# A two-layer decoder trunk on one core: squares of the new x in PSUM, one slab fetched ahead, and a bias copy cut in eight and moved

## The chip, the cores and the metric

The kernel runs on one core of a Trainium2 chip. The metric is the time of the program on the device in microseconds (us), smaller is better. The kernel before ran three times; its median is 1198.24 us.

## What is computed

Two decoder layers on 512 tokens of width 1024, in float32. Layer 0 mixes tokens with an indexer's sparse attention, layer 1 with a sliding window of 128 keys and sinks. Each is followed by a SwiGLU feed-forward part of width 2816, and the whole ends in a norm. One table of relative-position biases serves both mixers.

```python
def rms_norm(x, g):
    xf = x.astype(jnp.float32)
    y = xf * lax.rsqrt(jnp.mean(xf * xf, axis=-1, keepdims=True) + EPS)
    return (y * g.astype(jnp.float32)).astype(x.dtype)
...
    for layer in range(DEPTH):
        h = rms_norm(x, attn_norm[layer])
        if layer % N_MIXERS == 0:
            x = x + dsa_mixer(h, a_w_in[j], a_latent_norm[j], a_w_uv[j], a_w_out[j], rel_bias)
        else:
            x = x + swa_mixer(h, b_w_in[j], b_b_in[j], b_sinks[j], b_w_out[j], b_b_out[j], rel_bias)
        h = rms_norm(x, ffn_norm[layer])
        x = x + swiglu(h, ffn_w_gate_up[layer], ffn_w_down[layer])
    return rms_norm(x, final_norm)
```

## The kernel before

**Layout.** x is held transposed in SBUF, as 8 tiles of 128 features by 512 tokens, m = 0 to 7. Each float32 product is made of three TensorE products of 128x128 by 128x512: hi times hi, lo times hi and hi times lo (`mm3`, L570 to L572), where hi is the value rounded to fp32r and lo the rest.

**Slabs.** Weights come in 100 slabs, numbered in the order of use, into the two slots of `raw` (slot n % 2). SyncE (SP) issues each as two DMAs (`slab`, L308 and L309). Before it does, it waits on `lo_done` until the slab two before has been split. ScalarE (ACT) makes `w_hi` of a slab (`split_half`, L1043) once it has landed and the `w_hi` slot is free, GpSimd (POOL) makes `w_lo` (L461), and TensorE (PE) then has two output tiles of it (`unit_done`). A slab of the down products gives half a tile. Names: `S_F0` = 15 and `S_F1` = 62 are the first slabs of the gate and up products, `S_BK` = 53 holds layer two's keys and values, `S_BQ` = 54 to 57 its queries, `S_BO` = 58 to 61 its output projection. All of these DMAs go through SP's one queue, in the order in which SP issues them.

**Seams.** Between two parts of a layer the new x is made tile by tile. For each m VectorE (DVE) adds PE's result to x (L1605 and L1617 for the two output projections, L1654 for the down products), ACT makes `xs_hi` = x times gain (L1058) and the square of x (L1064, into `sq_mem` in SBUF), and DVE makes `xs_lo` (L1400) and adds the square to `ss` (L1409). PE starts the next part with `first_tiles`, which takes `xs_lo` m by m, and then `norm_sum` (L618) sums `ss` over the partitions. In the first norm, on the input, the squares go to PSUM instead (L1104, L1447). ACT, DVE and POOL run each program strictly in order. In the seam after the down products of layer 0, ACT splits slab 54 (`S_BQ`) before it makes `xs_hi` of m = 7. SP waits until PE has ended all down products (`unit_done`, `U_BK`) before it issues `sink` (L408), because `sink` lies where `act_hi` lay, and slab 54 is issued after that.

**The bias in DRAM.** `bias_row` holds one row of 1024 values per head. Skewed copies of it, DRAM to DRAM, make `bias_toep`, 128 rows of 512 values for each of the 16 heads. For layer 0 SP issues four copies of 4 heads (L381), between slabs. For layer 1, whose rows have 256 values, it issues one copy of all 16 heads (L402), between the last slab of layer 0's output projection and `S_F0`. Layer 1's attention reads from it two heads at a time into `b_toep` (`pair_in`, L421): DVE's `b_lowest` (L1740) takes `b_toep` and PE's logits, ACT takes the exponents. The attention runs over k = 0 to 7, two heads each. PE does, in this order, `b_logits(k)` (L579), the transposes of k - 2 (`b_turn`, L914 and L917), and in halves the query product of k + 2 (`b_project`). `b_logits(k)` waits until `b_lowest(k - 1)` has emptied its PSUM banks.

```python
            sp.wait_ge(neg_done, 4 * H)
            skew_b = bass.AP(tensor=bias_row.tensor, offset=ROW_A + P - 1, ap=[[GLEN, H], [-1, P], [1, 2 * P]])
            sp.dma_start(bias_toep[:, :, 0:2 * P], skew_b).then_inc(toep_out, 16)
            feed_forward(0, S_F0, S_D0)
...
            sp.wait_ge(toep_out, 32)
            pair_in(0)
```

Of the kernel before, what the change touches and what calls it, by code (L numbers as in the profile page):

```python
# [7 lines left out]
F32 = mybir.dt.float32  # L8
F32R = mybir.dt.float32r
ALU = mybir.AluOpType  # L10
ACT = mybir.ActivationFunctionType

P = 128
D = 1024
T = 512
DM = D // P
NB = T // P
FF = 2816
FT = FF // P
H = 16  # L20
R = 128
DH = 64
# [16 lines left out]
ROW_A, ROW_B = 640, 384  # L39
GLEN = ROW_A + ROW_B  # L40
# [4 lines left out]
U_A1, U_A2, U_AO, U_F0, U_D0 = 0, 6, 22, 30, 74  # L45
U_BK, U_BQ, U_BO, U_F1, U_D1, U_END = 90, 92, 100, 108, 152, 168
SLOT = 2048
KD = FT // 2
CUT_WIDE, CUT_DOWN = (1024, 2048), (768, KD * P)

# [13 lines left out]
    return value  # L64

SQ_BANK = (4, 5, 7)
B_OUT_BANK = (4, 1, 2, 3, 0, 1, 2, 3)

def is_down(n):
# [19 lines left out]
def trunk(nc, x_in, rel_bias, par_in, a_w_in, a_w_uv, a_w_out, b_w_in, b_sinks, b_w_out,  # L89
          w_gate_up, w_down, consts, bias_row, bias_toep, out):  # L90
    ctx = ExitStack()
    with ctx:
        def sb(name, shape, dt=F32, where=ctx):
            return where.enter_context(nc.sbuf_tensor(name, shape, dt))

        def sem(name):
            return ctx.enter_context(nc.semaphore(name))
# [25 lines left out]
        ss = sb("ss", [P, T])  # L123
# [87 lines left out]
        fm = ExitStack()  # L211
        act_hi = sb("act_hi", [P, FT, T], F32R, fm)
        act_lo = sb("act_lo", [P, FT, T], F32R, fm)
        gate = sb("gate", [P, T], F32, fm)
        up = sb("up", [P, T], F32, fm)
        glu = sb("glu", [P, 2, T], F32, fm)
# [11 lines left out]
        GAIN = [G_ATTN[0], G_FFN[0], G_ATTN[1], G_FFN[1]]  # L228

        raw_full = [sem("raw_full0"), sem("raw_full1")]  # L230
        hi_done, lo_done = sem("hi_done"), sem("lo_done")
        unit_done = sem("unit_done")
        id_in, tab_in, small_in, sink_in = sem("id_in"), sem("tab_in"), sem("small_in"), sem("sink_in")
# [53 lines left out]

        def pieces(buf, n):

            if S_BQ <= n < S_BO:  # L290
                if buf is raw:
                    v = buf[:, n % 2, :].rearrange("p (k a j c) -> p a k j c", k=DM, a=2, j=2)
                else:
                    v = buf[:, n % 2, :].rearrange("p (k j a c) -> p a k j c", k=DM, a=2, j=2)
                return [v[:, a, :, :, :] for a in range(2)]
            cut = CUT_DOWN if is_down(n) else CUT_WIDE
            return [buf[:, n % 2, 0:cut[0]], buf[:, n % 2, cut[0]:cut[1]]]
# [4 lines left out]
        def _(sp):  # L302
            def slab(n, it, src):

                for dst, s in src(n % 2):
                    if n >= 2:

                        sp.wait_ge(lo_done, 2 * (n - 1) + 4 * it)  # L308
                    sp.dma_start(dst, s).then_inc(raw_full[n % 2], 16)  # L309
# [28 lines left out]
            def feed_forward(layer, s_gu, s_d):  # L338

                w = w_gate_up[layer]  # L340
                with sp.Fori(0, FT // 2) as i:
                    for v in range(2):
                        slab(s_gu + v, i, two_halves(w, (2 * i + v) * P, (2 * i + v) * P + FF))
                with sp.Fori(0, DM) as m:
                    for c in range(2):
                        slab(s_d + c, m, down(w_down[layer], c, m))

# [48 lines left out]
                toep_in(h)  # L396
            for n in range(S_AO + 2, S_F0):
                slab(n, 0, wide(a_w_out[0], (n - S_AO) * 256))

            sp.wait_ge(neg_done, 4 * H)  # L400
            skew_b = bass.AP(tensor=bias_row.tensor, offset=ROW_A + P - 1, ap=[[GLEN, H], [-1, P], [1, 2 * P]])
            sp.dma_start(bias_toep[:, :, 0:2 * P], skew_b).then_inc(toep_out, 16)  # L402
            feed_forward(0, S_F0, S_D0)

            slab(S_BK, 0, wide(b_w_in[0], H * DH))

            sp.wait_ge(unit_done, U_BK)
            sp.dma_start(sink[:, :], b_sinks[0:1, :].broadcast_to([P, H])).then_inc(sink_in, 16)  # L408
# [1 line left out]
            for n in range(S_BQ, S_BO):  # L410
                c0 = (n - S_BQ) * 2 * DH
                slab(n, 0, two_halves(b_w_in[0], c0, c0 + H // 2 * DH))

            def pair_in(j):

# [16 lines left out]
                                 b_w_out[0, a * 512:(a + 1) * 512, c0:c0 + 256]  # L432
                                 .rearrange("(k p) n -> p k n", p=DH)).then_inc(raw_full[n % 2], 16)

            sp.wait_ge(toep_out, 32)
            pair_in(0)
            pair_in(1)
            bo_slab(S_BO)
# [588 lines left out]
        def _(act):  # L1027
# [5 lines left out]
            def split_half(n, half, it=0, after=0):  # L1033
                if half == 0 and n == 0:

                    act.wait_ge(raw_fore, 32)
                elif half == 0 or n == 0:

                    act.wait_ge(raw_full[n % 2], 32 * (n // 2 + 1) + 32 * it)
                    if n >= 2:  # L1040

                        act.wait_ge(unit_done, after)
                nc.scalar.copy(pieces(w_hi, n)[half], pieces(raw, n)[half]).then_inc(hi_done, 1)  # L1043
# [5 lines left out]
            def new_x(e, m, par, gain=None):  # L1049

                c = DM * e + m
                n0 = held(act, c + 1)
                n1 = held(act, c - 1)
                act.wait_ge(tab_in, TAB)

                act.wait_ge(x_new, n0)
                if gain is not None:
                    nc.scalar.activation(xs_hi_m(m), x[:, m, :], ACT.Copy,  # L1058
                                         scale=params[:, bass.ds(gain + m, 1)]).then_inc(xhi_done, 1)
                if e > 0 or m >= 2:  # L1060

                    act.wait_ge(tab_in, TAB)
                    act.wait_ge(ss_done, n1)
                nc.scalar.activation(sq[:, par, :], x[:, m, :], ACT.Square).then_inc(sq_done, 1)  # L1064

            def xs_hi_m(m):
                return xs_hi[:, bass.ds(m * T, T)]
# [322 lines left out]
        def _(dve):  # L1390
# [3 lines left out]
            def new_x(e, m, par, gain=None):  # L1394
# [11 lines left out]
                if not (isinstance(c, int) and c == 0):  # L1406

                    dve.wait_ge(ss_done, c)
                nc.vector.tensor_tensor(ss[:, :], ss[:, :], sq[:, par, :], ALU.add).then_inc(ss_done, 1)  # L1409

            def norm(e):

# [399 lines left out]
```

## Time and profile before

| | before |
|---|---|
| runs | 1200.09, 1198.24, 1195.34 us; median 1198.24 |
| the profiled execution: its own time | 1199.46 us |
| its span, first to last instruction | 1197.7 us |
| PE busy | 1164.0 us (97%) |
| DVE busy | 563.3 us (47%) |
| ACT busy | 457.8 us (38%) |
| POOL busy | 613.7 us (51%) |
| mean granted TensorE clock | 0.994 |

The span is the time between the first and the last instruction. The device time is 1.8 us longer. Busy times are sums over the whole span. The PE figure counts modelled ends of pipelined matmuls. A matmul is shown with a duration of about 390 ns, while one starts about every 0.23 us.

### The profile page before, as it was taken

What the parts mean: (1) busy time and instruction counts of PE and PEld (TensorE: products, weight loads), DVE (VectorE), ACT (ScalarE), POOL (GpSimd) and SP (SyncE); (2) the same over time, 40 slices, a digit from 0 to 9 for tenths busy, and PEclk for the clock granted to TensorE, in tenths of its full rate; (3) what the DMA queues carried; (4) which work ended last, traced back from release to release, by engine and by line L of the source; (5) the groups of instructions that cost most, each with busy time, mean ns of one, the idle gap of its engine ahead of it and who ended that gap; (6) DMA issues with size and microseconds to landing.
All of it is one profiled execution on the core that took longest, in us unless ns stands there. A gap on an engine that the chain in (4) does not pass through costs nothing.

```text
span 1197.7 us, 16046 instructions
## 1 busy us (share of the span) xinstructions
PE 1164.0 (97%) x5600; PEld 963.0 (80%) x5600; DVE 563.3 (47%) x927; ACT 457.8 (38%) x849; POOL 613.7 (51%) x359
## 2 busy tenths in 40 slices
PE   7999999999999999999999999999999999999996
PEld 5767889987788888888888778887888888888885
DVE  5379867745644434442222476647444444421111
ACT  5343257752422332223222376634323322332232
POOL 4435757864444544444444487834445444534441
PEclk9999999999999999999999999999999999999998
DMA  7531401118333233322332442313332333233221
GB/s 209 173 134 53 141 27 48 51 55 157 106 105 97 79 104 105 97 71 82 96 96 83 119 102 58 76 36 106 106 103 76 101 105 103 65 92 97 86 83 71
DMA packets 181283, 112.46 MB, mean 94 GB/s; under 512 B 7308, under 2 KB 175559, under 8 KB 181240
## 3 DMA queue, kind: packets, MB, share of 16 engines
q1 hardware_dynamic: 180512, 110.68, 33.2%
q10 hardware_dynamic: 728, 1.22, 0.3%
q8 instruction: 25, 0.41, 0.1%
q14 instruction: 18, 0.15, 0.0%
HBM read 109.72 MB, written 8.45 MB: 99 GB/s over the span
## 4 chain that ended last, share of the span: by engine, by line
PE 81%; DVE 5%; issue 4%; ACT 3%; DMA 2%; POOL 1%; ACTq 0%; SPq 0%; DVEq 0%
PE ps L570 26%; PE ps L572 25%; PE ps L571 25%; DVE ss L1409 2%; DMA raw<-in_ffn_w_gate_up 2%; PE ps L579 2%; PE ps L785 1%; ACT w_hi L1043 1%; DVE work L1505 1%; PE ps L914 1%; PE ps L764 1%; POOL w_lo L461 1%; DVE work L1489 1%; ACT xs_hi L1058 1%; DMA raw<-in_b_w_in 1%
## 5 line engine op out<-in xcount | busy, mean ns | idle before, releaser
L461 POOL TENSOR_TENSOR w_lo<-raw,w_hi 128x1024 fp32r<-128x1024 f32 (+1 forms) x200 | 462.7, 2335 | 497.5 <-ACT w_hi L1043 488.9
L570 PE MATMUL ps<-xs_hi,w_hi 128*128 128x512 f32 (+3 forms) x1024 | 399.3, 390 | 7.8 <-DVE xs_lo L1400 2.5
L572 PE MATMUL ps<-xs_hi,w_lo 128*128 128x512 f32 (+3 forms) x1024 | 394.8, 386 | 0.0
L571 PE MATMUL ps<-xs_lo,w_hi 128*128 128x512 f32 (+3 forms) x1024 | 394.6, 385 | 0.0
L1043 ACT CAST w_hi<-raw 128x1024 fp32r<-128x1024 f32 (+1 forms) x196 | 178.9, 962 | 433.8 <-PE ps L572 414.1
L570 PEld LDWEIGHTS ps<-xs_hi,w_hi 128*128 128x128 f32 x1024 | 192.5, 188 | 53.4 <-DVE xs_lo L1400 3.8
L571 PEld LDWEIGHTS ps<-xs_lo,w_hi 128*128 128x128 f32 x1024 | 192.6, 188 | 38.8 <-issue 1.1
L572 PEld LDWEIGHTS ps<-xs_hi,w_lo 128*128 128x128 f32 x1024 | 192.4, 188 | 38.8
L570 PE MATMUL ps<-act_hi,w_hi 128*128 128x512 f32 x352 | 139.2, 396 | 0.0
L572 PE MATMUL ps<-act_hi,w_lo 128*128 128x512 f32 x352 | 138.0, 392 | 0.0
L571 PE MATMUL ps<-act_lo,w_hi 128*128 128x512 f32 x352 | 136.6, 388 | 0.0
L1637 DVE TENSOR_TENSOR glu<-std,up 128x512 f32<-128x512 f32 x44 | 67.7, 1540 | 77.0 <-ACT std L1232 76.8
L1640 DVE TENSOR_TENSOR act_lo<-glu,act_hi 128x512 f32 (+1 forms) x44 | 76.2, 1731 | 41.5 <-ACT act_hi L1237 41.5
L1633 DVE TENSOR_TENSOR up<-ps,rstd 128x512 f32<-128x512 f32 x44 | 30.4, 692 | 138.7 <-PE ps L572 138.7
L1654 DVE TENSOR_TENSOR x<-ps,x 128x512 f32 x16 | 11.1, 692 | 175.0 <-PE ps L572 175.0
L572 PEld LDWEIGHTS ps<-act_hi,w_lo 128*128 128x128 f32 x352 | 66.1, 188 | 15.5
L571 PEld LDWEIGHTS ps<-act_lo,w_hi 128*128 128x128 f32 x352 | 66.1, 188 | 14.5
L570 PEld LDWEIGHTS ps<-act_hi,w_hi 128*128 128x128 f32 x352 | 66.2, 188 | 13.0
L553 POOL TENSOR_SCALAR b_prob<-b_prob,b_rinv 128x128 f32<-128x128 f32 (+1 forms) x64 | 54.1, 870 | 11.2 <-DVE b_rinv L1718 11.1
L1409 DVE TENSOR_TENSOR ss<-ss,sq_mem 128x512 f32<-128x512 f32 x32 | 55.2, 1725 | 9.8 <-ACT sq_mem L1064 9.8
L1237 ACT CAST act_hi<-glu 128x512 f32 (+1 forms) x44 | 27.4, 622 | 76.9 <-DVE glu L1637 76.9
L1400 DVE SCALAR_TENSOR_TENSOR xs_lo<-x,params,xs_hi (+1 forms) x24 | 25.4, 1060 | 49.0 <-ACT xs_hi L1058 49.0
(182 smaller groups left out, 1361.0 us busy)
## 6 DMA issues: line engine op xcount, KB each, us to landing
raw<-in_ffn_w_gate_up SPq DMA_DIRECT2D x88, 512.0 KB, 4.9
raw<-in_ffn_w_down SPq DMA_DIRECT2D x32, 384.0 KB, 3.6
raw<-in_a_w_in SPq DMA_DIRECT2D x20, 512.0 KB, 4.9
raw<-in_ffn_w_down SPq DMA_DIRECT2D x32, 320.0 KB, 4.0
raw<-in_b_w_in SPq DMA_DIRECT2D x10, 512.0 KB, 5.1
bias_toep<-bias_row SPq DMA_DIRECT2D x4, 1024.0 KB
toep<-bias_toep SPq DMA_DIRECT2D x16, 256.0 KB, 2.6
raw<-in_a_w_out SPq DMA_DIRECT2D x8, 512.0 KB, 4.3
```

The lines of the kernel that those rows point to most:

```text
L461: nc.gpsimd.tensor_tensor(pieces(w_lo, n)[half], pieces(raw, n)[half], pieces(w_hi, n)[half].bitcast(F32), ALU.subtract)\
L553: nc.gpsimd.tensor_scalar(at, at, b_rinv[:, k % 2, a, i:i + 1], None, ALU.mult)\
L570: nc.tensor.matmul(dst, wh, xh, start=start, stop=False, **kw)
L571: nc.tensor.matmul(dst, wh, xl, start=False, stop=False, **kw)
L572: return nc.tensor.matmul(dst, wl, xh, start=False, stop=stop, **kw)
L1043: nc.scalar.copy(pieces(w_hi, n)[half], pieces(raw, n)[half]).then_inc(hi_done, 1)
L1237: nc.scalar.copy(act_hi[:, j + 2 * it, :], glu[:, j % 2, :]).then_inc(ah_done, 1)
L1400: nc.vector.scalar_tensor_tensor(xs_lo[:, bass.ds(m * T, T)], x[:, m, :], params[:, bass.ds(gain + m, 1)], xs_hi[:, bass.ds(m * T, T)].bit ...
L1409: nc.vector.tensor_tensor(ss[:, :], ss[:, :], sq[:, par, :], ALU.add).then_inc(ss_done, 1)
L1633: nc.vector.tensor_tensor(up[:, :], ps[:, b + 1, :], rstd[:, :], ALU.mult).then_inc(up_done, 1)
L1637: nc.vector.tensor_tensor(glu[:, v, :], silu[:, :], up[:, :], ALU.mult).then_inc(glu_done, 1)
L1640: nc.vector.tensor_tensor(act_lo[:, v + 2 * it, :], glu[:, v, :], act_hi[:, v + 2 * it, :].bitcast(F32), ALU.subtract)\
```

## The change

Three things, at the places where one part of a layer follows another.

- The squares of the new x go to two banks of PSUM (`NORM_SQ`, a pair for each of the four norms) instead of `sq_mem`, and DVE adds them to `ss` from there.
- Slab 53 (`S_BK`) is fetched into a buffer of its own, `raw_next`, which lies where the feed-forward part's `gate`, `up` and `glu` lay. It is issued after the down slabs of the first three m, and slab 55 then waits for slab 51 instead of slab 53.
- The copy of `bias_row` for layer 1 leaves its place ahead of `S_F0`. It is cut into eight copies of two heads, two behind each of the slabs 54 to 57. SP waits for all eight before `pair_in(0)`.

```diff
--- before.py
+++ after.py
@@ -45,6 +45,7 @@
 U_A1, U_A2, U_AO, U_F0, U_D0 = 0, 6, 22, 30, 74
 U_BK, U_BQ, U_BO, U_F1, U_D1, U_END = 90, 92, 100, 108, 152, 168
 SLOT = 2048
+AHEAD = 3
 KD = FT // 2
 CUT_WIDE, CUT_DOWN = (1024, 2048), (768, KD * P)
 
@@ -64,6 +65,7 @@
     return value
 
 SQ_BANK = (4, 5, 7)
+NORM_SQ = {1: (4, 5), 2: (2, 3), 3: (5, 7), 4: (2, 3)}
 B_OUT_BANK = (4, 1, 2, 3, 0, 1, 2, 3)
 
 def is_down(n):
@@ -211,6 +213,9 @@
         fm = ExitStack()
         act_hi = sb("act_hi", [P, FT, T], F32R, fm)
         act_lo = sb("act_lo", [P, FT, T], F32R, fm)
+        next_m = ExitStack()
+        raw_next = sb("raw_next", [P, SLOT], F32, next_m)
+        next_m.close()
         gate = sb("gate", [P, T], F32, fm)
         up = sb("up", [P, T], F32, fm)
         glu = sb("glu", [P, 2, T], F32, fm)
@@ -228,6 +233,7 @@
         GAIN = [G_ATTN[0], G_FFN[0], G_ATTN[1], G_FFN[1]]
 
         raw_full = [sem("raw_full0"), sem("raw_full1")]
+        raw_ahead = sem("raw_ahead")
         hi_done, lo_done = sem("hi_done"), sem("lo_done")
         unit_done = sem("unit_done")
         id_in, tab_in, small_in, sink_in = sem("id_in"), sem("tab_in"), sem("small_in"), sem("sink_in")
@@ -287,6 +293,8 @@
 
         def pieces(buf, n):
 
+            if buf is raw and n == S_BK:
+                return [raw_next[:, 0:CUT_WIDE[0]], raw_next[:, CUT_WIDE[0]:CUT_WIDE[1]]]
             if S_BQ <= n < S_BO:
                 if buf is raw:
                     v = buf[:, n % 2, :].rearrange("p (k a j c) -> p a k j c", k=DM, a=2, j=2)
@@ -303,7 +311,10 @@
             def slab(n, it, src):
 
                 for dst, s in src(n % 2):
-                    if n >= 2:
+                    if n == S_BK + 2:
+
+                        sp.wait_ge(lo_done, 2 * (S_BK - 1))
+                    elif n >= 2:
 
                         sp.wait_ge(lo_done, 2 * (n - 1) + 4 * it)
                     sp.dma_start(dst, s).then_inc(raw_full[n % 2], 16)
@@ -341,7 +352,18 @@
                 with sp.Fori(0, FT // 2) as i:
                     for v in range(2):
                         slab(s_gu + v, i, two_halves(w, (2 * i + v) * P, (2 * i + v) * P + FF))
-                with sp.Fori(0, DM) as m:
+                for m in range(AHEAD):
+                    for c in range(2):
+                        slab(s_d + c, m, down(w_down[layer], c, m))
+                if layer == 0:
+                    v = raw_next[:, :].rearrange("p (k n) -> p k n", k=DM)
+                    g = b_w_in[0].rearrange("(k p) n -> p k n", p=P)
+
+                    sp.wait_ge(al_done, FT)
+                    for i in range(2):
+                        sp.dma_start(v[:, 4 * i:4 * i + 4, :], g[:, 4 * i:4 * i + 4, H * DH:H * DH + 256])\
+                            .then_inc(raw_ahead, 16)
+                with sp.Fori(AHEAD, DM) as m:
                     for c in range(2):
                         slab(s_d + c, m, down(w_down[layer], c, m))
 
@@ -396,13 +418,7 @@
                 toep_in(h)
             for n in range(S_AO + 2, S_F0):
                 slab(n, 0, wide(a_w_out[0], (n - S_AO) * 256))
-
-            sp.wait_ge(neg_done, 4 * H)
-            skew_b = bass.AP(tensor=bias_row.tensor, offset=ROW_A + P - 1, ap=[[GLEN, H], [-1, P], [1, 2 * P]])
-            sp.dma_start(bias_toep[:, :, 0:2 * P], skew_b).then_inc(toep_out, 16)
             feed_forward(0, S_F0, S_D0)
-
-            slab(S_BK, 0, wide(b_w_in[0], H * DH))
 
             sp.wait_ge(unit_done, U_BK)
             sp.dma_start(sink[:, :], b_sinks[0:1, :].broadcast_to([P, H])).then_inc(sink_in, 16)
@@ -410,6 +426,13 @@
             for n in range(S_BQ, S_BO):
                 c0 = (n - S_BQ) * 2 * DH
                 slab(n, 0, two_halves(b_w_in[0], c0, c0 + H // 2 * DH))
+                if n == S_BQ:
+
+                    sp.wait_ge(neg_done, 4 * H)
+                for h in (2 * (n - S_BQ), 2 * (n - S_BQ) + H // 2):
+                    skew_b = bass.AP(tensor=bias_row.tensor, offset=h * GLEN + ROW_A + P - 1,
+                                     ap=[[GLEN, 2], [-1, P], [1, 2 * P]])
+                    sp.dma_start(bias_toep[h:h + 2, :, 0:2 * P], skew_b).then_inc(toep_out, 16)
 
             def pair_in(j):
 
@@ -432,7 +455,7 @@
                                  b_w_out[0, a * 512:(a + 1) * 512, c0:c0 + 256]
                                  .rearrange("(k p) n -> p k n", p=DH)).then_inc(raw_full[n % 2], 16)
 
-            sp.wait_ge(toep_out, 32)
+            sp.wait_ge(toep_out, 64 + 8 * 16)
             pair_in(0)
             pair_in(1)
             bo_slab(S_BO)
@@ -1036,7 +1059,10 @@
                     act.wait_ge(raw_fore, 32)
                 elif half == 0 or n == 0:
 
-                    act.wait_ge(raw_full[n % 2], 32 * (n // 2 + 1) + 32 * it)
+                    if n == S_BK:
+                        act.wait_ge(raw_ahead, 32)
+                    else:
+                        act.wait_ge(raw_full[n % 2], 32 * (n // 2 + 1 - (n > S_BK and n % 2)) + 32 * it)
                     if n >= 2:
 
                         act.wait_ge(unit_done, after)
@@ -1061,7 +1087,7 @@
 
                     act.wait_ge(tab_in, TAB)
                     act.wait_ge(ss_done, n1)
-                nc.scalar.activation(sq[:, par, :], x[:, m, :], ACT.Square).then_inc(sq_done, 1)
+                nc.scalar.activation(ps[:, NORM_SQ[e][par], :], x[:, m, :], ACT.Square).then_inc(sq_done, 1)
 
             def xs_hi_m(m):
                 return xs_hi[:, bass.ds(m * T, T)]
@@ -1406,7 +1432,7 @@
                 if not (isinstance(c, int) and c == 0):
 
                     dve.wait_ge(ss_done, c)
-                nc.vector.tensor_tensor(ss[:, :], ss[:, :], sq[:, par, :], ALU.add).then_inc(ss_done, 1)
+                nc.vector.tensor_tensor(ss[:, :], ss[:, :], ps[:, NORM_SQ[e][par], :], ALU.add).then_inc(ss_done, 1)
 
             def norm(e):
 
```

On SP, ahead of the gate and up slabs of layer 0, the order before is this (`L402` is the copy of 16 heads, its rows times values stand behind the names):

```order
L389 DMA toep<-bias_toep 128x512 x14
L309 DMA raw<-in_a_w_out 128x4x256 x4
L402 DMA bias_toep<-bias_row 2048x1x256
L341 UNCONDITIONAL_BRANCH
L341 ISA
L309 ISA
L309 DMA raw<-in_ffn_w_gate_up 128x8x128
```

In the changed kernel the same place reads:

```order
L411 DMA toep<-bias_toep 128x512 x14
L320 DMA raw<-in_a_w_out 128x4x256 x4
L352 UNCONDITIONAL_BRANCH
L352 ISA
L320 ISA
L320 DMA raw<-in_ffn_w_gate_up 128x8x128
```

The copy is gone from between the two kinds of slabs. The second place is SP after the down products of layer 0, before:

```order
L309 DMA raw<-in_b_w_in 128x4x256 x2
L408 DMA sink<-in_b_sinks 128x16
L309 DMA raw<-in_b_w_in 128x8x128 x8
L421 DMA b_toep<-bias_toep 128x256 x4
L431 DMA raw<-in_b_w_out 64x8x256 x2
```

and in the changed kernel:

```order
L424 DMA sink<-in_b_sinks 128x16
L320 DMA raw<-in_b_w_in 128x8x128 x2
L435 DMA bias_toep<-bias_row 256x1x256 x2
L320 DMA raw<-in_b_w_in 128x8x128 x2
L435 DMA bias_toep<-bias_row 256x1x256 x2
L320 DMA raw<-in_b_w_in 128x8x128 x2
L435 DMA bias_toep<-bias_row 256x1x256 x2
L320 DMA raw<-in_b_w_in 128x8x128 x2
L435 DMA bias_toep<-bias_row 256x1x256 x2
```

Slab 53 has moved up into the down products. Slab 54 still stands behind `sink`, and each query slab is now followed by two copies. `pair_in` follows behind the last of them.

## Rows read from the trace of the kernel before

**Rows 1.** The page, busy time and instructions of each engine.
```profile
PE 1164.0 (97%) x5600; PEld 963.0 (80%) x5600; DVE 563.3 (47%) x927; ACT 457.8 (38%) x849; POOL 613.7 (51%) x359
```
**Rows 2.** Waits of PE over the span: us in total, times, longest.
```profile
PE ps L570 <- DVE xs_lo L1400: 2.5, 2, 1.5
PE ps L570 <- DVE x L1605: 1.8, 1, 1.8
PE ps L618 <- DVE ss L1409: 1.1, 1, 1.1
```
**Rows 3.** Chain of waits, 255 to 320 us: start, us, what.
```profile
273.68 18.74 DMA raw<-in_ffn_w_gate_up
```
**Rows 4.** Timeline, SP, ACT and PE, first seam: start, us, instruction, idle before.
```profile
267.34 0.60 SPq L402 DMA_DIRECT2D bias_toep<-bias_row  x1
...
292.52 2.00 ACT L1043 CAST w_hi<-raw 128x1024 fp32r<-128x1024 f32 x2 [7.12 <-DMA raw<-in_ffn_w_gate_up]
...
300.06 0.51 PE L570 MATMUL ps<-xs_hi,w_hi 128*128 128x512 f32 x1 [1.75 <-DVE x L1605]
...
310.91 0.50 PE L570 MATMUL ps<-xs_hi,w_hi 128*128 128x512 f32 x1 [1.03 <-DVE xs_lo L1400]
```
**Rows 5.** Instructions on the tile ss: duration ns min/median/max, first and last start.
```profile
L1409 DVE TENSOR_TENSOR ss<-ss,sq_mem x32: 683/1676/2890, 269.4 to 1186.5; 128x512 f32<-128x512 f32 x32
L1447 DVE TENSOR_TENSOR ss<-ss,ps x8: 687/687/690, 24.9 to 30.4; 128x512 f32<-128x512 f32 x8
```
**Rows 6.** Timeline, SP and ACT, seam after the down products.
```profile
655.36 2.00 ACT L1043 CAST w_hi<-raw 128x1024 fp32r<-128x1024 f32 x2 [4.95 <-PE ps L572]
...
663.23 23.58 SPq L309 DMA_DIRECT2D raw<-in_b_w_in  x8
...
669.73 2.00 ACT L1043 CAST w_hi<-raw 128x1024 fp32r<-128x1024 f32 x2 [12.37 <-DMA raw<-in_b_w_in]
...
679.91 1.98 ACT L1043 CAST w_hi<-raw 128x1024 fp32r<-128x1024 f32 x2
...
688.75 1.99 ACT L1043 CAST w_hi<-raw 128x1024 fp32r<-128x1024 f32 x2 [0.85 <-PE ps L572]
```
**Rows 7.** The page, DMA issues of the copies: count, KB each.
```profile
bias_toep<-bias_row SPq DMA_DIRECT2D x4, 1024.0 KB
...
bias_toep<-bias_row SPq DMA_DIRECT2D x1, 2048.0 KB
```
**Rows 8.** Timeline, SP, first and last of the four copies of 4 heads.
```profile
28.38 0.80 SPq L381 DMA_DIRECT2D bias_toep<-bias_row  x1
...
63.25 2.37 SPq L381 DMA_DIRECT2D bias_toep<-bias_row  x1
```
**Rows 9.** Windows with these copies; the last columns are granted clock, DMA share, GB/s.
```profile
42.00:52.00 10.00, 9.29 (x40) 6.79 (x40) 4.41 (x8) 4.05 (x6) 4.76 (x2) 1.00 0.27 101
...
69.00:80.00 11.00, 11.00 (x57) 7.05 (x58) 6.63 (x8) 6.75 (x12) 5.21 (x3) 1.00 0.26 101
...
81.00:82.00 1.00, 1.00 (x8) 0.59 (x8) 1.00 (x1) 0.24 (x1) 0.69 (x1) 1.00 0.67 130
```
**Rows 10.** Windows with the copy of 16 heads, and with slabs 54 and 55.
```profile
272.00:287.00 15.00, 15.00 (x67) 12.29 (x67) 9.50 (x11) 5.63 (x8) 5.23 (x2) 1.00 1.03 129
...
664.00:672.00 8.00, 8.00 (x37) 6.57 (x36) 0.00 (x0) 2.27 (x3) 1.14 (x1) 1.00 1.02 254
```
**Rows 11.** Timeline, SP, DVE and PE, start of layer 1's attention.
```profile
686.85 2.72 SPq L421 DMA_DIRECT2D b_toep<-bias_toep  x4
...
693.42 0.34 DVE L1740 CUSTOM_DVE_ANT_0 b_prob<-ps,b_toep,nsink 128x128 f32<-128x128 f32 x1
...
697.47 0.33 PE L579 MATMUL ps<-bk_hi,bq_hi 64*128 64x128 f32 x2
```
**Rows 12.** Landing time of the DMAs of L421, all 16.
```profile
DMA to landing us min/median/max: 1.9/2.4/6.1
```
**Rows 13.** A window behind two gaps of PE (1.1 and 1.9 us).
```profile
764.00:768.00 4.00, 3.33 (x10) 2.67 (x10) 2.85 (x9) 1.98 (x9) 4.00 (x6) 0.58 0.97 194
```

## The prediction

> **What bounds the kernel now.** I began with the busy times: PE is busy 97% of the span [rows 1], so a stage gets faster only where PE's gaps get shorter, and any new gap of PE is added to the time in full. Then I read who makes PE wait [rows 2]. The places that this change touches cost 1.75 and 1.03 us in the seam before layer 0's feed-forward part [rows 4] and 1.1 us at `norm_sum` in the seam after the down products (third row of [rows 2]). That is all the change can win, 3.9 us. The chain of waits names the cause of the first seam: the first gate and up slab took 18.74 us from issue to landing [rows 3], because the bias copy of 16 heads was issued just ahead of it [rows 4]. ACT stood still 7.12 us for that slab, and the `xs_hi` behind it came late. Last I read the DMA shares, for what the copies do to the queue [rows 7 to 10].
>
> **Part 1, squares in PSUM.** Adding a square from `sq_mem` took 0.68 to 2.89 us on DVE, and 0.69 us in all 8 cases where the square was in PSUM [rows 5]. The slow ones lie beside POOL's subtractions. I take 0.69 for all 32. It saves DVE time in every seam, but PE feels it in one place alone, the 1.1 us at `norm_sum`. I count that at nothing, for a reason given in part 3: what comes after it waits for a DMA that starts at a fixed point before it. ACT's write to PSUM changes place only, and I count it at nothing; four banks that PE does not use at that time hold the squares.
>
> **Part 2, slab 53 ahead.** ACT's split of slab 53 did not wait for a DMA but for PE to free the `w_hi` slot (the cast at 655.36, [rows 6]). So the earlier fetch has nothing to shorten. The wait of this seam is ACT's 12.37 us for slab 54 (the cast at 669.73, [rows 6]), which is issued at 663.23 because SP waits for the end of the down products first. The order of SP in the changed kernel still has slab 54 behind `sink`, so this wait stays, and with it `xs_hi` of m = 7, which stands behind the split. I count the part at nothing. Its cover is ample: slab 53's two DMAs go in among the down slabs.
>
> **Part 3a, the copy leaves the first seam.** With nothing ahead of it the first gate and up slab lands long before ACT could take it, since PE frees the `w_hi` slot only about 5.5 us before the cast at 292.52. ACT then has `xs_hi` of m = 4 some 5 us earlier, and DVE is no longer late with x of m = 5. At the end of the seam `xs_lo` of m = 7 is needed after 42 products of the seven earlier m. PE starts one per 0.224 us (67 in 15.00 us [rows 10]), so 9.4 us after it starts at about 298, and it is ready about 7 us after that start. Both gaps go: **2.8 us won**. Nothing is late next there.
>
> **Part 3b, eight copies of two heads between the query slabs.** This is the term that decides.
>
> How many DMA engines does one copy use? A copy of 4 heads ran at a DMA share of 0.27 [rows 9], which is 4 of 16 engines. The copy of 16 heads ran at 1.03 [rows 10], all of them. One engine per head: a copy of 2 heads should use 2.
>
> Are they always the same ones? The four copies of 4 heads were issued from 28.38 to 63.25 [rows 8]. Each moved 1 MB [rows 7] at 101 GB/s [rows 9], so took 10.4 us. Had the last copy had engines of its own, it would have been over by about 63.3 + 4 + 10.4 = 78 us, and it would have added its share to that of the third. But the share stayed at 0.26 and never 0.5 in 69 to 80 us, and the stream ended in the window of 81 to 82 [rows 9]. Four copies in a row (42 us) and the parts of three slabs between them (3 us each) starting at 28.9 end at 80 us. So the copies take turns on the same engines, and a slab's part on those engines waits behind them.
>
> What does a copy of 2 heads take? An engine has 128 rows of 1 KB. A 2 KB row took 10.4 us / 128 = 81 ns. Slabs 54 and 55, in 512 byte rows, had 256 rows per engine in some 7.1 us [rows 10], 28 ns each. Between the two on a straight line 1 KB takes 46 ns, and a copy **5.8 us**. The lower bound is half of the 10.4 us, 5.2; the upper one the full 10.4, if the cost is per row. Further off lies the copy of 16 heads: 2.1 MB at 129 GB/s [rows 10] is 16.3 us for 128 rows of 1 KB on each engine. I take 5.8 because two engines are nearer to four than to sixteen, and four showed no crowding.
>
> The Trainium skill (DMA: Bandwidth & Descriptors, Specifications) says that an engine moves about 27 GiB/s and that transfers of 512 B or more run at line rate. By that a copy would take an estimated 4.5 us and the sum below would be 10 us less; the 16.3 us of the 16 heads speak against using it as it stands.
>
> The two engines then work without a break from 664.9, some 1.7 us after slab 54's issue [rows 6]: four slabs of 3.6 us (two in 7.1 us, as above) and eight copies of 5.8 us, 60.8 us, until 725.7. With 1.2 us for the last landing and its semaphore, SP passes its wait at 726.9. Two DMAs of `pair_in(0)` take 0.7 us to issue (a quarter of 2.72 each [rows 11]) and 2.4 us to land [rows 12]: `b_lowest(0)` starts at 730.0 instead of 693.4 [rows 11]. PE's `b_logits(1)` needs all but the last 0.8 us of its 3.1 us, so starts at 732.3 instead of 697.5 [rows 11]: **34.9 us lost** (34.8 and a little for the semaphore). All on the path: behind `b_logits(1)` PE has nothing else it may do, and PE was busy before.
>
> Other waits in that stretch are hidden by this one. Slab 55 lands at about 684.5 on the two engines (664.9 + 3.6 + 11.6 + 3.6 = 683.7) where ACT wanted it at 679.9, and slab 56 at about 700 where ACT wanted it at 688.75 [rows 6]. ACT has `kv`, the queries and the exponents queued behind these splits, PE the first logits, POOL its splits. All are done by 730. That is also why the 1.1 us of part 1 wins nothing: the queue of the two engines starts at the end of the down products, ahead of `norm_sum`.
>
> **Part 4, the clock.** Behind gaps of 1.1 and 1.9 us the granted clock was 0.58 in the next 4 us [rows 13], near the lower level of 1.2 GHz, which costs 1.7 us of work at full rate. A gap of some 30 us will do this at least once: **1.7 us lost**.
>
> **Sum.** Own time of the profiled execution 1199.5 - 2.8 + 34.9 + 1.7 = 1233.3. That execution lies 1.2 us above the median of the runs, so the forecast is **1232 us**. With copies of 5.2 us it is 1227, with copies of 10.4 us 1269. The parts of slabs and the moment of the start may be off by 4 us below that.
>
> **Rivals.**
>
> *All sixteen engines serve each copy (not slower).* A DMA of 2 heads might be cut finer than by heads. Then a pair of copies, 0.5 MB at 129 GB/s, takes 4.1 us. Slab 57 cannot be issued before 685.8, when slab 55 is split; the queue then ends slab 57 at 691.6 and its copies at 695.7, and `b_lowest(0)` starts at 700.0, 6.6 us late. PE had 1.8 us to spare, so loses 4.8: 1199.5 - 2.8 + 4.8 - 1.2 = 1200. It decides if the share in the copies is above 0.5. Against it is the 0.27 of four heads.
>
> *The copies run at the pace of slabs on all engines.* A pair takes 2 us. The last still stands behind slab 57, so `b_lowest(0)` starts at about 697, and PE loses 1.7: 1197. This is the best case; it shows that even then the change wins about 1 us, since the last pair is issued where `pair_in(0)` was before [rows 11]. Against it is that no copy from DRAM to DRAM went above 129 GB/s.
>
> *Copies as slow as the 16 heads.* 8 x 16.3 us instead of 46.4 adds 84 us: 1316. The same 1 KB rows speak for it, that only two engines work speaks against.
>
> *The change does not do what it says.* For slab 53 this is my forecast, in part 2. Were I wrong, and slab 54 came earlier, 1.5 us of PE's wait for `xs_lo` would go (part of the first row of [rows 2]), but it would not be seen behind the wait for the copies.
>
> One page speaks to the first two rivals, apart from the rows. The Trainium skill (DMA: Bandwidth & Descriptors, Why a DMA increments its semaphore by 16 and not by 1) says that a DMA gets the largest number of engines up to 16 that divides the slowest dimension of both its sides, and the lowest-numbered ones. That makes 4 for 4 heads, which the share of 0.27 agrees with, and it would make 2 for 2 heads, which no run yet shows.
>
> **How the numbers follow.** The forecast's case (two fixed engines, copies of 5.2 to 10.4 us) has 0.84, the slow copies 0.03, all engines 0.07, the pace of slabs 0.06. The range is that of the first case, 1223 to 1269, and holds 0.82. A measurement of this kernel can tell about 0.5%, 6 us, from no change. Slower by more than that: 0.84 + 0.03 = 0.87. Within it: 0.11 of the two middle rivals. Faster by over 0.5%: 0.02, since even the best case wins 1 us.
>
> **What would show it.** In the changed profile: adding the squares takes 0.69 us throughout; ACT's wait of 7.12 us and PE's gaps of 1.75 and 1.03 us are gone; PE reaches layer 0's last down product about 2.8 us earlier. Then, from about 670 to 723 us, the DMA share is near 0.13 with short peaks for slabs, SP waits for `toep_out` into the 720s, and PE has one gap of about 30 us ahead of `b_logits(1)`, with a clock near half behind it. It is wrong if the share in the copies is above 0.2, or if the queue is empty at 700 us.

## The result, and the profile after

The changed kernel takes 1223.74 us (median of 4 runs, 1222.44 to 1225.37), the kernel before 1197.28 in the same comparison. The ratio is 1.0219, with a 95% interval of 1.0198 to 1.0240: slower by about 26 us. The forecast was 1232, with a range of 1223 to 1269 us: the measured time lies in it, 0.7 us above its lower end.

| | before | after |
|---|---|---|
| the profiled execution: its own time | 1199.46 | 1225.04 |
| its span | 1197.7 | 1223.2 |
| PE busy | 1164.0 | 1164.0 |
| DVE busy | 563.3 | 529.9 |
| mean granted TensorE clock | 0.994 | 0.984 |

The page of the changed kernel, busy time of each engine, answers to [rows 1]:

```profile
PE 1164.0 (95%) x5600; PEld 964.2 (79%) x5600; DVE 529.9 (43%) x927; ACT 457.1 (37%) x849; POOL 610.5 (50%) x359
```

PE does the same work in the same busy time, so the 25.5 us of span are gaps, nearly all of them in one place. Who makes PE wait, in us in total, times and longest, answers to [rows 2]:

```profile
PE ps L602 <- DVE b_low L1766: 27.2, 2, 26.2
...
PE ps L602 <- DVE bq_lo L1715: 4.2, 1, 4.2
```

The three waits of [rows 2] that the change could reach are gone, but for 1.67 us at `xs_lo` in the seam after the down products (1.46 before). One gap of 26.2 us has come, ahead of `b_logits(1)`, and 4.2 us ahead of `b_logits(0)` where there were 1.1. In sum: 26.2 + 3.1 + 0.2 more, 1.75 + 1.03 + 1.1 less, which is 25.6 us. The chain of waits through it (start, us, what):

```profile
685.64 8.36 DMA raw<-in_b_w_in
694.02 1.06 ACT w_hi L1069
...
704.91 13.78 DMA bias_toep<-bias_row
718.70 0.34 SPq L444
719.08 2.30 DMA b_toep<-bias_toep
...
723.94 2.93 PE ps L602 x24
```

Read it backwards: PE's logits wait for DVE, DVE for `b_toep`, SP's issue of that for the last bias copy, which took 13.78 us from issue to landing. Windows in which the copies alone moved data, but for the last rows of slab 54 in the first (granted clock, DMA share, GB/s last), beside [rows 9, 10]:

```profile
666.00:672.00 6.00, 4.33 (x19) 3.27 (x19) 1.85 (x2) 3.10 (x4) 4.15 (x2) 1.00 0.14 50
...
706.00:718.00 12.00, 0.00 (x0) 0.00 (x0) 0.00 (x0) 0.00 (x0) 0.00 (x0) 0.50 0.14 48
```

A share of 0.14 is 2.2 of 16 engines, and 256 KB at 48 GB/s take 5.5 us. Both copies of a pair had been issued in these windows, and the share stays at 0.14 where two at a time would show 0.28: they took turns on the same two engines. SP's timeline shows a second effect (start, us from the first to the last of the group):

```profile
661.12 5.15 SPq L435 DMA_DIRECT2D bias_toep<-bias_row  x2
666.32 8.28 SPq L320 DMA_DIRECT2D raw<-in_b_w_in  x2
674.64 5.60 SPq L435 DMA_DIRECT2D bias_toep<-bias_row  x2
680.28 8.03 SPq L320 DMA_DIRECT2D raw<-in_b_w_in  x2
688.35 5.60 SPq L435 DMA_DIRECT2D bias_toep<-bias_row  x2
694.00 8.36 SPq L320 DMA_DIRECT2D raw<-in_b_w_in  x2
702.39 5.60 SPq L435 DMA_DIRECT2D bias_toep<-bias_row  x2
718.70 1.29 SPq L444 DMA_DIRECT2D b_toep<-bias_toep  x3
```

A group starts every 14 us, which is two copies and a slab's part on the two engines. The two DMAs of a slab took some 8 us to issue, where those of slab 54 took 1 (660.03 to 661.08). In the first window above, SP stood in the issue of slab 55 and the share was 0.14: SP was held up behind the copies, and the other 14 engines got nothing either. How much the queue takes before SP stands still, the runs do not show.

### The profile page after: what moved, and what is told of

Same layout as the page of the kernel before. It is cut to its first block, busy times and chain, and to the rows that moved or that the text cites. A ratio compares the mean times of both kernels' runs of the same rounds, so it can differ in the third digit from the quotient of the medians.

```text
span 1223.2 us, 15995 instructions
## 1 busy us (share of the span) xinstructions
PE 1164.0 (95%) x5600; PEld 964.2 (79%) x5600; DVE 529.9 (43%) x927; ACT 457.1 (37%) x849; POOL 610.5 (50%) x359
## 4 chain that ended last, share of the span: by engine, by line
PE 84%; DMA 3%; DVE 3%; issue 2%; POOL 1%; ACT 1%; SPq 0%; ACTq 0%; DVEq 0%
PE ps L593 27%; PE ps L595 26%; PE ps L594 26%; DMA raw<-in_b_w_in 2%; PE ps L602 1%; PE ps L808 1%; POOL w_lo L484 1%; DMA bias_toep<-bias_row 1%; DVE work L1531 1%; PE ps L937 1%; PE ps L787 1%; DVE work L1515 1%; PE ps L940 0%; DVE xs_lo L1418 0%; ACT w_hi L1069 0%
## 5 line engine op out<-in xcount | busy, mean ns | idle before, releaser
L484 POOL TENSOR_TENSOR w_lo<-raw,w_hi 128x1024 fp32r<-128x1024 f32 (+1 forms) x198 | 454.7, 2318 | 499.6 <-ACT w_hi L1069 491.1
L1426 DVE SCALAR_TENSOR_TENSOR xs_lo<-x,params,xs_hi (+1 forms) x24 | 25.6, 1067 | 59.1 <-ACT xs_hi L1084 59.1
L1766 DVE CUSTOM_DVE_ANT_0 b_prob<-ps,b_toep,nsink 128x128 f32<-128x128 f32 (+1 forms) x64 | 25.1, 447 | 39.1 <-DMA b_toep<-bias_toep 22.8
```

Source lines behind the costliest of these rows:

```text
L484: nc.gpsimd.tensor_tensor(pieces(w_lo, n)[half], pieces(raw, n)[half], pieces(w_hi, n)[half].bitcast(F32), ALU.subtract)\
L1426: nc.vector.scalar_tensor_tensor(xs_lo[:, bass.ds(m * T, T)], x[:, m, :], params[:, bass.ds(gain + m, 1)], xs_hi[:, bass.ds(m * T, T)].bit ...
L1766: nc.vector.tensor_tensor_reduce(out=b_prob[:, par, a, OFFB[i]:OFFB[i] + n], in0=ps[:, 2 * a + i // 2, c0:c0 + n], in1=b_toep[:, par, a, 2 ...
```

## Experiments

Times are medians of several runs, with the interval of the ratio to the kernel before where it matters. Runs of one kernel lie up to 10 us apart. Therefore I also give the stretch from the PE product behind PE's wait for `xs_lo` at about 240 us into the span to the last `y_turn`, in the profiled execution. It leaves out the start of the program, which differed by up to 4 us between executions. Before it is 946.4 us (240.73 to 1187.09), after 972.3 (240.86 to 1213.19). Part of a difference between two stretches, 1.6 us, can be TensorE's clock late in the program and not the edit (last section); where it matters, I say so.

### The cut: 4 heads per copy

```diff
-                for h in (2 * (n - S_BQ), 2 * (n - S_BQ) + H // 2):
-                                     ap=[[GLEN, 2], [-1, P], [1, 2 * P]])
+                h = 4 * (n - S_BQ)
+                                 ap=[[GLEN, 4], [-1, P], [1, 2 * P]])
```

> The changed kernel with four copies of 4 heads in place of eight of 2, one behind each query slab; the same bytes at the same place. Theory (each copy has one engine per head, always the same ones, and runs at 24 GB/s per engine): share 0.27 in the copies, 4 x 5.5 us instead of 8 x 5.5 us of queue; the queue then ends soon after slab 57, at about 696 us, and PE's gap ahead of b_logits(1) shrinks from 26 us to about 4: 1202 us. Rival (2 MB from DRAM to DRAM among the slabs costs what it costs, however it is cut): 1220 to 1224 us.

Measured: 1203.9 us (ratio 1.0034 to 1.0071). PE's gap ahead of `b_logits(1)` was 9.1 us, not 4. A window with the last copy, the last rows of slab 57 ahead of it:

```profile
691.00:697.00 6.00, 2.95 (x14) 2.10 (x12) 0.00 (x0) 0.00 (x0) 0.53 (x1) 1.00 0.28 95
```

The share and the pace per engine (95 / 4 = 24 GB/s) are as the theory has them. The same bytes at the same place cost 20 us less, so the rival falls. The gap is larger than I expected because slab 57 goes out only at about 685 and the last copy behind it, so `pair_in(0)` was issued at 697.9.

### The cut: 8 heads per copy

```diff
+                if n % 2 == 0:
+                    h = 4 * (n - S_BQ)
+                                     ap=[[GLEN, 8], [-1, P], [1, 2 * P]])
```

> The changed kernel with two copies of 8 heads, behind slabs 54 and 56, in place of eight of 2. The same bytes. Theory (one engine per head, 128 rows of 1 KB on each whatever the number of heads, so a copy takes as long as one of 2 or 4 heads unless engines crowd each other): share about 0.55, each 5.5 to 8 us. The queue ends by about 690 us; PE's gap is 2 to 4 us: 1195 to 1199 us, between the run with 4 heads (1203.9) and the run by rows (1196.2).

Measured: 1196.93 us (0.9968 to 1.0005), as the theory has it; a gap of 1.0 us ahead of `b_logits(1)`, less than expected, and 2.8 ahead of `b_logits(0)`. The window with the second copy:

```profile
682.00:686.00 4.00, 3.50 (x18) 2.71 (x16) 2.62 (x2) 1.28 (x3) 3.41 (x2) 1.00 0.54 167
```

Eight heads, 8.6 engines, 21 GB/s on each. One engine per head once more.

### The cut: all heads, by rows

```diff
+                for p0 in (32 * (n - S_BQ), 32 * (n - S_BQ) + 16):
+                    skew_b = bass.AP(tensor=bias_row.tensor, offset=ROW_A + P - 1 - p0,
+                                     ap=[[GLEN, H], [-1, 16], [1, 2 * P]])
+                    sp.dma_start(bias_toep[:, p0:p0 + 16, 0:2 * P], skew_b).then_inc(toep_out, 16)
```

> The changed kernel with the eight copies cut by rows: all 16 heads, 16 rows each. The same bytes, number and places. Theory: share near 1.0 in the copies, a copy in about 2 us; the last one lands near 693 to 696 us, PE's gap is 2 to 5 us: 1197 to 1201 us. Rival (the place among the slabs is what costs): 1220 us or more.

Measured: 1196.15 us (0.9976 to 1.0010), gap 2.0 us. Its ten runs lie between 1191.6 and 1201.3, and the profiled one was the fastest; why they differ more than others is open. Windows with the first, the second and the last pair of copies:

```profile
663.00:664.00 1.00, 1.00 (x6) 0.84 (x5) 0.00 (x0) 0.39 (x1) 0.00 (x0) 1.00 1.19 317
...
671.00:673.00 2.00, 2.00 (x10) 1.65 (x9) 1.99 (x1) 1.99 (x3) 0.71 (x1) 1.00 0.98 99
...
684.00:685.00 1.00, 1.00 (x10) 0.78 (x8) 1.00 (x1) 0.41 (x2) 1.00 (x2) 1.00 1.13 358
```

This has the same number of copies, of the same size, at the same places as the change; only the slowest dimension is 16 heads instead of 2, with 16 rows of each instead of 128. It is 27.6 us faster. The place among the slabs is not what costs those 27.6 us. All 16 engines are at work in these windows, but at very different paces: 317 and 358 GB/s, and 99 in between, 6 on each engine where 2 engines had 24 each. Why the pace falls so far within one run is open. So 16 engines can be faster than 8 (167 GB/s) or slower.

### No second copy

```diff
-                    sp.dma_start(bias_toep[h:h + 2, :, 0:2 * P], skew_b).then_inc(toep_out, 16)
-            sp.wait_ge(toep_out, 64 + 8 * 16)
+            sp.wait_ge(toep_out, 64)
```

> The changed kernel without the second bias copy: layer 1's attention reads the rows that layer 0's copies left, which leaves that copy out. It prices everything else in the change. Theory: no gap ahead of b_logits(1), the first seam's gaps of 1.75 and 1.03 us gone and now also the 1.1 us at norm_sum: 1192 to 1194 us. Rival (slab 53 ahead or the squares in PSUM cost something themselves): 1197 us or more.

Measured: 1190.63 us (0.9911 to 0.9956), 1.4 us below the theory's range; a stretch of 939.6 us. That is the change with no second copy at all, neither in the old place nor in the new one. The copies in their new form and place cost 33 us against it. Cut by rows they still cost 2.0 us by the stretch (941.6, its late clock the same), which is PE's gap of 2.0 us there.

### Is it SP's wait, or the place in the queue?

```diff
-            sp.wait_ge(toep_out, 64 + 8 * 16)
...
+                if j % 2 == 0:
+                    sp.wait_ge(toep_b[j // 2], 32)
```

> The changed kernel, its copies of 2 heads and their places kept, but each pair of copies has a semaphore of its own, and pair_in(j) waits only for the two copies that it reads, instead of for all eight. Theory A (the gap is the wait for all eight): what is left is set by slab 56, which lands behind four copies on the two engines, so ACT's split of it is at 694 us as in the changed kernel and b_lowest(0) can start at about 699: PE's gap is about 4 us, total 1202 us. Theory B (the slabs' own lateness behind the copies is most of the loss): slabs 56 and 57 hold PE up through the first half of the attention, 1210 to 1224 us.

Measured: 1226.24 us. The gap ahead of `b_logits(1)` was still 24.5 us (us in total, times, longest):

```profile
PE ps L604 <- DVE b_low L1768: 25.6, 2, 24.5
```

Neither theory is right. SP no longer waited for the last copies, and issued `pair_in(0)` at 707.5, but (timeline of SP and DVE):

```profile
701.85 5.60 SPq L436 DMA_DIRECT2D bias_toep<-bias_row  x2
707.50 6.74 SPq L447 DMA_DIRECT2D b_toep<-bias_toep  x4
...
720.16 0.35 DVE L1768 CUSTOM_DVE_ANT_0 b_prob<-ps,b_toep,nsink 128x128 f32<-128x128 f32 x1 [21.94 <-DMA b_toep<-bias_toep]
```

`b_toep` landed at 720 all the same. My reading was that it is spread over all engines and that its parts on the two stood behind all eight copies: not the semaphore held it, but the order in the queue. The next run tests that.

```diff
+                if n == S_BQ + 2:
+                    pair_in(0)
+                    pair_in(1)
```

> The changed kernel with a semaphore for each pair of copies, and with pair_in(0) and pair_in(1) issued ahead of the two copies behind slab 56, not behind all eight. Theory (what held pair_in(0) in the run before was not SP's wait but its place in the queue: its own parts on the two engines stood behind all copies): b_toep of k = 0 is there at about 694 us, PE's gap ahead of b_logits(1) falls to about 4 us; then pair_in(2), still behind the last copies, holds b_lowest(2) until about 720 us and costs PE 5 to 6 us more: about 1206 us. Rival (something else in the stretch, such as late slabs, holds PE): 1215 us or more.

Measured: 1217.53 us, some 11 more than the theory said. PE's timeline, its two gaps:

```profile
698.55 0.47 PE L605 MATMUL ps<-bk_hi,bq_hi 64*128 64x128 f32 x2 [2.44 <-DVE b_low L1769]
...
726.61 0.45 PE L940 MATMUL ps<-tab,b_prob 128*128 128x128 f32 x1 [12.38 <-DVE bpt_lo L1421]
```

The first gap fell from 24.5 to 2.4 us, as forecast: that `pair_in(0)` was held by its place in the queue is shown. The total lies in the rival's range (1215 or more), though PE's second gap is again a wait for `b_toep`. The second is `pair_in(2)`, still behind the last copies. It was late by more than I had reckoned, because SP stood issuing again, and issued it from 714.49 on:

```profile
701.38 5.95 SPq L451 DMA_DIRECT2D bias_toep<-bias_row  x2
707.37 7.01 SPq L460 DMA_DIRECT2D raw<-in_b_w_out  x2
714.49 17.46 SPq L436 DMA_DIRECT2D b_toep<-bias_toep  x6
```

DVE waited 14.3 us for that `b_toep`. What late slabs alone would cost was not measured apart.

### The other two parts

```diff
-                nc.scalar.activation(sq[:, par, :], x[:, m, :], ACT.Square).then_inc(sq_done, 1)
+                nc.scalar.activation(ps[:, NORM_SQ[e][par], :], x[:, m, :], ACT.Square).then_inc(sq_done, 1)
```

That and its counterpart on DVE, in the kernel before:

> The kernel before with the squares in PSUM as its only change. Theory: adding a square takes 0.69 us on DVE throughout; the 1.1 us at norm_sum go, the gap of 1.75 us in the first seam goes too (DVE is late there only by the 2.9 us of one addition), the 1.03 us stay or shrink: 1194 to 1196 us, where the kernel before has 1198. Rival (no effect outside DVE): 1198 us.

Measured: 1191.68 us (0.9934 to 0.9970), 2.3 us below the theory's range; a stretch of 941.8. The squares alone win 5.3 us by the medians and 4.5 by the stretch. In the first seam (timelines of ACT and PE):

```profile
292.52 2.00 ACT L1044 CAST w_hi<-raw 128x1024 fp32r<-128x1024 f32 x2 [10.07 <-DMA raw<-in_ffn_w_gate_up]
...
297.87 0.50 PE L571 MATMUL ps<-xs_hi,w_hi 128*128 128x512 f32 x1 [0.27 <-DVE x L1606]
```

The slab is as late as before, and ACT waits even longer for it, yet PE's gap has shrunk from 1.75 to 0.27 us and the second one is gone.

```diff
+            skew_b = bass.AP(tensor=bias_row.tensor, offset=ROW_A + P - 1, ap=[[GLEN, H], [-1, P], [1, 2 * P]])
+            sp.dma_start(bias_toep[:, :, 0:2 * P], skew_b).then_inc(toep_out, 16)
             feed_forward(0, S_F0, S_D0)
```

> The changed kernel with the one copy of 16 heads back at its old place ahead of the first gate and up slab; squares in PSUM and slab 53 ahead stay. Theory (slab 53 ahead is worth nothing): the same time as the kernel with the squares alone, within 1 us: 1194 to 1196 us. Rival (slab 53 ahead has a price or a gain of its own): it differs from that kernel by over 2 us.

Measured: 1192.22 us (0.9927 to 0.9970), a stretch of 941.7. The total is below the range again, for the reason of the run before. Against the squares alone it is 0.5 us in the medians and 0.1 in the stretch: slab 53 ahead is worth nothing that can be told.

And the kernel before without the second copy, its squares still in SBUF:

> The kernel before, squares still in SBUF, without its second bias copy (layer 1's attention reads layer 0's rows, which leaves that copy out). The squares alone removed PE's gaps of 1.75 and 1.03 us with the copy still there. Theory A (either remedy is enough: the gaps need both a late slab and a slow addition): both gaps are gone here too, the 1.1 us at norm_sum stay: about 1195 us, 2.8 below the kernel before. Theory B (only the slow additions made the gaps): they stay, 1197 to 1198 us.

Measured: 1194.03 us (0.9952 to 0.9980), both gaps of the first seam gone, the 1.1 us at `norm_sum` still there:

```profile
PE ps L614 <- DVE ss L1405: 1.1, 1, 1.1
```

So the gaps need both, a late slab and a slow addition, and either remedy is enough, but for the 0.27 us that the squares alone leave.

### A version that beats both

The copies by rows stand among the first six down slabs of layer 0, and slabs 54 and 55 are issued ahead of SP's wait for the end of the down products:

```diff
                 for m in range(AHEAD):
                     for c in range(2):
                         slab(s_d + c, m, down(w_down[layer], c, m))
+                        if layer == 0:
+                            q = 2 * m + c
+                            for p0 in ((16 * q,) if q < 4 else (64 + 32 * (q - 4), 80 + 32 * (q - 4))):
+                                skew_b = bass.AP(tensor=bias_row.tensor, offset=ROW_A + P - 1 - p0,
+                                                 ap=[[GLEN, H], [-1, 16], [1, 2 * P]])
+                                sp.dma_start(bias_toep[:, p0:p0 + 16, 0:2 * P], skew_b).then_inc(toep_out, 16)
...
             for n in range(S_BQ, S_BO):
+                if n == S_BQ + 2:
+                    sp.wait_ge(unit_done, U_BK)
+                    sp.dma_start(sink[:, :], b_sinks[0:1, :].broadcast_to([P, H])).then_inc(sink_in, 16)
```

> The changed kernel with the copies cut by rows (16 heads, 16 rows each, so all engines) and issued among the first six down slabs of layer 0, and with slabs 54 and 55 issued ahead of the wait for the end of the down products, sink behind them. Theory: no gap ahead of b_logits(1), ACT does not wait for slab 54, PE's 1.4 us wait for xs_lo in that seam goes as well; some 8 us below the kernel before: 1188 to 1191 us. Rival (the copies hold up the down slabs, which are on PE's path): 1195 us or more.

Measured: 1188.87 us (median of 6), ratio 0.9926 (0.9902 to 0.9949), 35 us below the changed kernel. ACT's split of slab 54 waits for PE's slot and no longer for a DMA:

```profile
658.16 2.00 ACT L1070 CAST w_hi<-raw 128x1024 fp32r<-128x1024 f32 x2 [5.56 <-PE ps L596]
```

and PE has no gap in that seam before the 1.1 us ahead of `b_logits(0)`. Most of what it wins over the kernel before is the squares': against them alone it is 2.8 us less by the medians and 2.3 by the stretch (939.5 against 941.8, the late clock low in both). The run changes the form, the place of the copies and the time of slabs 54 and 55 together, and does not price them one by one.

## Why the prediction was right, and where its sizes were off

**The deciding term, right in kind, 5.6 us too large.** Two engines, always in turn, a share near 0.13, SP waiting for `toep_out` and one long gap ahead of `b_logits(1)`: all of it is in the profile. What was said to show it came earlier and smaller than said: SP's wait ended at 718.7 and not in the 720s, the gap is 26 us and not 30. The total is inside the range by 0.7 us only, and that is partly luck: with its own lower bound of 5.2 us for a copy, everything else as measured, the time would have fallen below it. Of the sizes:

- A copy took 5.5 us (256 KB at 48 GB/s), not 5.8. Eight of them: 2.7 us less.
- A slab's part on the two engines: the stream ran from about 661.5 to 718.2, 56.7 us; less 43.7 for the copies that leaves 3.2 us for each slab, not 3.6. Four of them: 1.4 us less. The 3.6 was read rightly, but with all sixteen engines at work (292 GB/s, 18 on each). A slab's part on the two engines, with nothing beside it, went at 43 GB/s, 21 on each, and would take 3.0 us. The windows, before and after:

```profile
667.00:672.00 5.00, 5.00 (x24) 4.13 (x22) 0.00 (x0) 2.27 (x3) 1.14 (x1) 1.00 1.19 292
...
678.00:679.00 1.00, 1.00 (x6) 0.84 (x5) 0.91 (x2) 0.00 (x0) 0.00 (x0) 1.00 0.14 43
```

- The rest of the 5.6 is in when the queue began and in the last landing, 0.6 and 0.7 us, and 0.2 in the steps behind it. For the last landing and its semaphore the forecast had 1.2 us without a row; it took 0.5. SP passed its wait at 718.7; by the forecast's steps it would have been 726.9 less the 2.8 of the first seam.

`b_logits(1)` started at 723.94 against 697.47 [rows 11], so 26.5 us later, 29.3 with the 2.8 won earlier. The forecast had 34.9. The 4.2 us ahead of `b_logits(0)` come from slab 55 (ACT waited 4.56 us for it) and, as forecast, are hidden: the copies set the time of `b_logits(1)`.

That the two engines are the same each time follows from the share of 0.14 with two copies issued, from the period of 14 us and from `b_toep` behind the copies. That they are the lowest-numbered ones, as the Trainium skill (DMA: Bandwidth & Descriptors, Why a DMA increments its semaphore by 16 and not by 1) has it, no row shows. Its rule for their number agrees with shares of 0.14, 0.28 and 0.54 for 2, 4 and 8 heads.

**Part 3a, the first seam: right.** Both gaps went, 2.8 us. ACT's split of the first gate and up slab in the changed kernel:

```profile
287.48 2.00 ACT L1069 CAST w_hi<-raw 128x1024 fp32r<-128x1024 f32 x2 [4.20 <-PE ps L595]
```

It waits for PE, not for the slab. But the squares would have closed these gaps by themselves, to 0.2 us in the run with the copy put back. Its stretch is 2.1 us above that of the kernel without the copy, and 1.6 of it is the late clock, so leaving the copy where it was would have cost about 0.5 us. The forecast credits the move with a gain that part 1 already holds.

**Part 1, the squares: right in the sum of this change, wrong as a price.** Adding a square took 0.67 to 0.69 us in all 32 cases. In this change the 1.1 us at `norm_sum` are lost again in the wait for the copies, as forecast. What failed is the step that PE feels the additions in one place alone: they were one of the two causes of the first seam's gaps as well. Alone the part is worth 4.5 (by the stretch) to 5.3 us (by the medians, 1197.01 and 1191.68), not 1.1. Of the 4.5, 2.5 lie in the first seam (1.75 + 1.03 - 0.27), 1.1 at `norm_sum`, and 0.3 in the seam behind layer 1's attention, which I had not counted because that gap is too short to be listed. The last 0.6 I could not place. So the forecast's ceiling, 3.9 us for all that the change can win, was too low as well: without the second copy the changed kernel is 7.2 us below the kernel before by the medians, and about 5 by the stretch once 1.6 us of clock are taken off. What it missed are delays too short to be listed as gaps, of which only the 0.3 us above are placed.

**Part 2, slab 53 ahead: right**, nothing, by the run with the copy put back. The wait for slab 54 is in the changed kernel as before, and the last experiment shows that issuing it earlier removes it:

```profile
666.72 2.00 ACT L1069 CAST w_hi<-raw 128x1024 fp32r<-128x1024 f32 x2 [12.59 <-DMA raw<-in_b_w_in]
```

**Part 4, the clock: right behind the long gap, and a surprise later.** The logits behind the 26 us gap took 2.93 us instead of 1.60, with this window:

```profile
723.00:728.00 5.00, 4.06 (x28) 3.69 (x29) 3.94 (x20) 4.87 (x20) 1.26 (x2) 0.55 1.10 216
```

By the next listed gap the changed kernel was 28.05 us behind instead of 26.5, so 1.6 us lost, where 1.7 were forecast. Then it got 2 us back in the second half (1.6 of clock and 0.3 of seam) and 0.6 at the very end. That and the 5.6 us make up the 8 us between 1233 and the profiled 1225.

**The rivals.** All sixteen engines, the pace of slabs, and copies as slow as the 16 heads are all excluded by the share of 0.14 and the 24 GB/s per engine. The run cut by rows is the case of the first, all engines: 1196, where 1200 was worked out with copies at 129 GB/s. What was held against the second, that no copy went above 129 GB/s, holds for the kernel before only: cut by rows, the last pair was in a window of 358. No run has copies at that pace throughout.

## What to carry to other kernels

Look at the slowest dimension of a DMA before cutting it: two heads of 128 rows use two engines, sixteen heads of 16 rows use all, with the same bytes, and the difference was 27.6 us here. A narrow DMA in a shared queue holds up every wide one behind it, by its parts on the same engines and by the issuing engine that stands still, so a finer semaphore alone does not help. When two causes make one gap, price each remedy alone before adding them up.

## What the runs showed that I had not expected

- SP took some 8 us to issue two DMAs of a slab behind two copies of 2 heads, against 1 us for the first slab.
- Copies from DRAM to DRAM ran at 24 GB/s per engine with 2 or 4 engines, 21 with 8, and with 16 at anything from 6 to 22 (99 to 358 GB/s in all, in windows of one run that hold some rows of slabs too).
- PE's gap of 1.9 us near the end of the attention was followed by the lower clock in some executions and not in others. In the changed kernel the same gap, with the same instructions around it, left the clock at 2.4 GHz. The stretch from there to the last `y_turn` was 422.4 us before (764.67 to 1187.09) and 420.5 after (792.73 to 1213.19). In the ten experiments it was near 422.1 in five and between 420.4 and 420.8 in the other five, and kernels with squares in PSUM are in both groups. So some 1.6 us of a difference between two profiled executions does not go with the squares or the copies, and looks like chance. That is not shown: no kernel was profiled in both ways. The windows from that gap on, of the kernel with the squares alone:

```profile
761.00:763.00 2.00, 2.00 (x9) 1.62 (x8) 0.96 (x3) 0.09 (x1) 2.00 (x3) 0.50 0.81 159
```

and of the changed kernel:

```profile
794.00:796.00 2.00, 2.00 (x15) 1.77 (x14) 1.45 (x4) 1.01 (x3) 2.00 (x3) 1.00 0.82 154
```
